# Moving snapshots and a copy ahead of the silus on ScalarE, squares of q and k into two homes, and two taps ahead of the joins

## The chip, the cores and the metric

The kernel runs on one core of one Trainium2 chip. The metric is the device time of one execution in microseconds (us); the number given for a version is the median of its runs. TensorE (PE) multiplies matrices into PSUM, VectorE (DVE), ScalarE (ACT) and GpSimd (POOL) work element by element, and SyncE (SP) issues most of the DMAs. All five run their own instruction streams in order and meet at semaphores.

## The reference, cut to what matters

Two transformer blocks follow each other on 512 latent tokens and 256 context tokens of width 1024, all in float32. The change touches the first layer of the first block alone, a gated delta rule in both directions (a "DeltaNet" mixer):

```
qkv = silu(centred_dwconv(p[..., :4096], conv_w))     # p = u @ w_in, five taps
z   = p[..., 4096:6144]
q, k = l2_norm(q), l2_norm(k)                         # 8 heads of 128, each used by two value heads
# chunks of 128 tokens here: invert (I + A), A strictly triangular; then scan over the chunks
o = rms_norm(o_forward + o_backward, o_norm_g)
y = (o * silu(z)) @ w_out
```

What follows it (attention, three kinds of attention in the second block, gates, a convolutional feed-forward part) is computed by code that the change leaves as it is.

## The kernel before, in words

**Layout.** Features lie on the 128 partitions and the 768 tokens along the row. The mixer is worked off in eight groups, j = 0 to 7; a group has one head of q, one of k and two of v, and two of z. A list of steps, written out by the generator `dn_order` (L259), is read by each engine's program, which picks from it the steps that it has a part in. The order of the list is therefore the order on every engine, and only semaphores move an engine against another. In the loop over j (L314) an iteration finishes group j and prepares group k = j + 1. It has three stretches.

**Stretch 1, products and solve (L322 to L361).** The projections are done by a fast scheme with seven products instead of eight, P1 to P7, for each pair of 128-row tiles (`pair_product`, L1329). Pair 0 of group k is q and k, pair 1 is its two v, pair 2 is the two z of group j. A product is eight matmuls of 385 columns. P1, P6, P7 and P4 add up in one PSUM bank: after each ScalarE copies the bank out (`pair_snap`, L2160), and the next of the four may not start before that copy is done. P2, P5, P7 and P3 also have an addition on VectorE (`pair_add`, L2759). In the same stretch ScalarE takes the square of the previous group's output (`osq`), the root of its mean (`sum_sq`, L2308), the silu of z (`zg`, L2212) and the silus of the two v tiles (`silu`, L2179); each of the two silu steps needs another table and loads back the one with Ln and Exp behind it. `gate_o` on VectorE scales the output by the root, and `finish` on TensorE transposes it (L1534). `blocks` (L2248) is a 96-row copy on ScalarE that waits for a DMA from DRAM (`blocks_in`, L1070), and VectorE's 15 steps `solve` (L2831) wait for it. `turn` transposes the two silued v tiles on TensorE, each followed by a copy on VectorE (L2797); the second transpose writes the same two banks and waits for the first copy.

**Stretch 2, joins (L399 to L403).** Nine rounds over six chunks: TensorE's small matmuls x, p and y for sizes 16, 32 and 64, each answered by copies or masks on ScalarE or VectorE. The list `behind` (L364) puts other work behind each round: the seven products of z, the 20 taps of the convolution of group k (`conv`, L2769, five for each of four tiles), the silu of q and k, and their norms. The norm of q (n = 0) and then of k (n = 1) is a square on VectorE (`norm_sq`, L2785), a sum over partitions on TensorE (`norm`, L1356), Ln and Exp on ScalarE (L2194) and a product on VectorE (`norm_x`, L2792). Both squares are written to the one buffer sqA, so k's square waits for q's sum.

**Stretch 3, scan (L419 to L448).** Six steps of a short chain between TensorE, VectorE and ScalarE, with the matrices of group k built beside it, and at its end P1 of the next group and the DMAs that bring group k's diagonal blocks to DRAM and back.

Of the kernel before, what the change touches and what calls it, by code (L numbers as in the profile page):

```python
# [16 lines left out]
LN_SET = "natural_log_exp_and_others"  # L17
# [241 lines left out]
def dn_order():  # L259
# [54 lines left out]
    for j in range(8):  # L314
# [5 lines left out]
            return [("pair_add", j, 2, name)]  # L320

        yield "clean", j  # L322
        if j:
            yield "zg", j - 1
        if j < 7:
            yield "silu", j, 2, 3
            yield from unit(k, 0, "P2") + unit(k, 0, "P6")
            if j:
                yield "sum_sq", j - 1
            yield "pair_add", k, 0, "P2"  # L330
            yield from unit(k, 0, "P5")
            yield "pair_add", k, 0, "P5"
            if j:
                yield "gate_o", j - 1
            yield from unit(k, 0, "P7")
            yield "pair_add", k, 0, "P7"
            yield "blocks", j
            yield from unit(k, 0, "P3")
            yield "solve", j, 1
            yield "pair_add", k, 0, "P3"  # L340
            yield from unit(k, 0, "P4")
            if j:
                yield "finish", j - 1
            for i in range(2, 9):
                yield "solve", j, i
            yield from unit(k, 1, "P1") + unit(k, 1, "P2") + unit(k, 1, "P6")
            for i in range(9, 16):
                yield "solve", j, i
            yield from unit(k, 1, "P5")
            yield "solved", j  # L350
            yield "pair_add", k, 1, "P2"
            if j:
                yield "fin_y", j - 1
            yield "turn", j, 0
            yield "turn", j, 1
            yield "pair_add", k, 1, "P5"
            yield from unit(k, 1, "P7")
            yield "pair_add", k, 1, "P7"
            yield from unit(k, 1, "P3")
            yield "pair_add", k, 1, "P3"  # L360
            yield from unit(k, 1, "P4")  # L361

            t = [x for n in range(4) for x in conv(k, n)]
            behind = [zh[:2] + t[:5], zh[2:4] + t[5:6], z_add("P2") + zh[4:7] + t[6:12],  # L364
                      [("silu", k, 0, 1)] + z_add("P5") + zh[7:10] + z_add("P7") + t[12:14], zh[10:12] + t[14:15],
                      z_add("P3") + zh[12:] + t[15:] + [("norm_sq", k, 0)],
                      [("norm", k, 0), ("norm_x", k, 0), ("norm_sq", k, 1)], [("norm", k, 1), ("norm_x", k, 1)], []]
            if k == 7:
                behind[8] = [("silu", 7, 2, 3), ("turn", 7, 0), ("turn", 7, 1)]
        else:  # L370


            p = [("mod_k", n, x) for n in (4, 5) for x in range(8)][1:] + zh
            out = [("out", 0, k, (0, 1)) for k in DN_OUT[:14]]
            behind = [p[27:], *(out[a:a + 2] for a in range(0, 14, 2)), []]
            behind[3] += [("zg", 7)]
            yield from p[:4]
            yield "sum_sq", 6
            yield "gate_o", 6
            yield "blocks", 7  # L380
            for i in range(1, 16):
                yield "solve", 7, i
                yield p[3 + i]
                if i == 2:
                    yield "finish", 6
                if i == 12:
                    yield "mod_turn", 4
                    yield "mod_turn", 5
                if i == 14:
                    yield "pair_add", 7, 2, "P2"  # L390
            yield "solved", 7
            yield "fin_y", 6
            yield from p[19:23]
            yield "pair_add", 7, 2, "P5"
            yield from p[23:25]
            yield "pair_add", 7, 2, "P7"
            yield from p[25:27]
            yield "pair_add", 7, 2, "P3"
# [127 lines left out]
def program(nc, D):  # L526

    ctx = ExitStack()
    with ctx:
# [83 lines left out]
        def raw_of(j, n):  # L613

            return conv_buf[(2 * (j % 3) + n) % 6]

        def conv_of(j, n):

# [558 lines left out]
        def tensor_program(e):  # L1177
# [176 lines left out]
                    leave_banks((f"pair_{event}", j, p), bank)  # L1354

            def norm(j, n):  # L1356
                e.wait_ge(*at("nrm_sq", j, n))
                take_banks(0, 1)
                e.matmul(ps[:, 0, :], ones, sqA[:, 0:512], start=True, stop=True)
                e.matmul(ps[:, 1, 0:256], ones, sqA[:, 512:768], start=True, stop=True).then_inc(*mark("nrm_pe", j, n))  # L1360
                leave_banks(("nrm_ln", j, n), 0, 1)

            def turn(j, h):
# [701 lines left out]
        def scalar_program(e):  # L2065
# [146 lines left out]
            def zg(j):  # L2212
                for event in ("c11", "c12", "c21", "c22"):
                    e.wait_ge(*at(f"pair_{event}", j, 2))
                e.activation(zg_of(j), zg_of(j), ACT.Silu).then_inc(*mark("z_silu", j))
                e.preload_act_table_set(LN_SET)

            def spread(j, c):

# [449 lines left out]
        def vector_program(e):  # L2669
# [115 lines left out]
            def norm_sq(j, n):  # L2785
                x = (qT, kT)[n][j % 2]
                e.wait_ge(*at("silu", j, n))
                if n:
                    e.wait_ge(*at("nrm_pe", j, 0))
                e.tensor_tensor(sqA, x, x, MUL).then_inc(*mark("nrm_sq", j, n))  # L2790

            def norm_x(j, n):  # L2792
                x = (qT, kT)[n][j % 2]
# [883 lines left out]
```

## Time and profile before

| | |
|---|---|
| median of 3 runs | 2994.41 us (2991.03 to 2996.15) |
| the profiled execution's own time | 2989.97 us |
| span of the profiled execution | 2988.2 us |
| mean granted TensorE clock | 0.973 of full speed |
| one iteration of the loop over j | 136.9 us (566.56 to 703.46, start of the same matmul group) |

Line numbers such as L1350 are lines of the kernel before. L2069 is the helper through which ScalarE copies, so snapshots, join copies and `blocks` all carry it; the shapes tell them apart (128x385 is a snapshot, 96x256 is `blocks` or `solved`). In a timeline a row is a group of equal instructions: its start, how long it lasted, and in brackets how long the engine had been idle before it and what it waited for. The "granted clock" of a stretch is 1.00 at 2.4 GHz and 0.50 at 1.2 GHz.

### The profile page before, as it was taken

How to read it: one execution, taken by the hardware profiler on the slowest of the kernel's cores; microseconds unless marked ns; L12 is line 12 of the kernel's file. 1: busy time of each engine (PE TensorE's matmuls, PEld its weight loads, DVE VectorE, ACT ScalarE, POOL GpSimd, SP SyncE). 2: the span in 40 equal slices, each digit the busy share in tenths (PEclk: the TensorE clock that was granted, in tenths of full speed). 3: DMA queues.
4: the chain of work that ended last, by engine and by line, in shares of the span. 5: the costliest groups of instructions: out<-in, count | busy, mean ns of one | idle time of the engine just before them, and what ended most of it. 6: DMA issues, size and time to landing. Idle time of an engine off the chain costs nothing.

```text
span 2988.2 us, 39117 instructions
## 1 busy us (share of the span) xinstructions
PE 2771.6 (93%) x15874; PEld 1910.7 (64%) x15874; DVE 1507.0 (50%) x3076; ACT 991.9 (33%) x2545; POOL 351.6 (12%) x268
## 2 busy tenths in 40 slices
PE   8798989898989979999999988999999999999998
PEld 3566666675757656764554434668776765588886
DVE  3565666666666653752333233543348421677733
ACT  1436364454636362202233222322224321211200
POOL 0220111101111110000000012123203220000031
PEclk9899999999999989999999999999999999999999
DMA  5110101111010114421100111111231211221220
GB/s 219 46 38 20 60 6 60 22 44 50 17 49 21 45 59 158 169 85 63 57 29 29 35 38 71 57 57 57 86 126 43 85 71 57 85 85 57 98 113 30
DMA packets 78132, 193.65 MB, mean 65 GB/s; under 512 B 56096, under 2 KB 61856, under 8 KB 66432
## 3 DMA queue, kind: packets, MB, share of 16 engines
q1 hardware_dynamic: 55520, 186.65, 17.3%
q10 hardware_dynamic: 22432, 4.49, 0.8%
q8 instruction: 126, 2.06, 0.3%
q14 instruction: 54, 0.44, 0.0%
HBM read 181.16 MB, written 9.96 MB: 64 GB/s over the span
## 4 chain that ended last, share of the span: by engine, by line
PE 81%; DVE 8%; ACT 8%; issue 1%; DMA 1%; ACTq 0%; SPq 0%; DVEq 0%
PE ps L1812 9%; PE ps L1350 9%; PE ps L2012 9%; PE ps L1264 7%; PE ps L1559 6%; PE ps L2040 4%; PE ps L1829 3%; PE ps L1952 3%; PE ps L1690 2%; DVE arena L2840 2%; ACT arena L2070 2%; PE ps L1418 2%; PE ps L1428 2%; PE ps L1440 2%; PE ps L1389 1%; PE ps L1702 1%
## 5 line engine op out<-in xcount | busy, mean ns | idle before, releaser
L2069 ACT ACTIVATE arena<-ps 64x64 f32<-64x64 f32 (+8 forms) x1011 | 320.3, 342 | 859.2 <-PE ps L1350 264.2
L1350 PE MATMUL ps<-arena 128*128 128x385 f32 x1232 | 431.4, 504 | 51.1 <-ACT arena L2069 51.1
L1350 PEld LDWEIGHTS ps<-arena 128*128 128x128 f32 x1232 | 234.4, 196 | 210.2 <-issue 69.6
L1812 PE MATMUL ps<-arena 128*128 128x256 f32 x1456 | 328.7, 380 | 2.0 <-ACT arena L2069 2.0
L1812 PEld LDWEIGHTS ps<-arena 128*128 128x128 f32 x1456 | 271.7, 191 | 40.2 <-issue 5.7
L2012 PE MATMUL ps<-arena 128*128 128x256 f32 x1176 | 254.7, 378 | 0.0
L2012 PEld LDWEIGHTS ps<-arena 128*128 128x128 f32 x1176 | 222.4, 189 | 32.5 <-issue 0.5
L1264 PE MATMUL ps<-arena 128*128 128x512 f32 x496 | 222.3, 607 | 14.7 <-DVE arena L3102 5.1
L1264 PEld LDWEIGHTS ps<-arena 128*128 128x128 f32 x496 | 96.0, 195 | 139.4 <-issue 130.2
L2070 ACT ACTIVATE arena<-ps,arena 128x128 f32<-128x128 f32 x544 | 157.1, 379 | 77.2 <-PE ps L1493 47.3
L1559 PE MATMUL ps<-arena 128*128 128x512 f32 (+1 forms) x512 | 170.3, 488 | 0.3 <-DVE arena L2931 0.3
L1559 PEld LDWEIGHTS ps<-arena 128*128 128x128 f32 x512 | 95.0, 189 | 64.9 <-issue 57.7
L2040 PE MATMUL ps<-arena 128*128 128x256 f32 x616 | 133.7, 379 | 1.2 <-DVE arena L3362 1.2
L2782 DVE SCALAR_TENSOR_TENSOR arena<-arena 128x770 f32<-128x770 f32 x128 | 131.2, 1025 | 3.8
L2040 PEld LDWEIGHTS ps<-arena 128*128 128x128 f32 x616 | 116.5, 189 | 18.2 <-DVE arena L3362 1.6
L2767 DVE TENSOR_TENSOR arena<-arena,ps 128x385 f32<-128x385 f32 x88 | 48.7, 553 | 147.4 <-ACT arena L2069 99.7
L2091 ACT ACTIVATE arena<-arena 128x768 f32<-128x768 f32 (+1 forms) x16 | 11.8, 737 | 259.0 <-DVE arena L3000 141.7
L2640 ACT ACTIVATE arena<-arena 128x512 f32<-128x512 f32 x44 | 33.4, 806 | 187.2 <-DVE arena L3346 187.2
L3506 POOL TENSOR_TENSOR arena<-arena 128x512 f32<-128x512 f32 x26 | 34.9, 1343 | 508.9 <-PE ps L1812 281.5
L2428 ACT ACTIVATE arena<-arena 128x128 f32<-128x128 f32 (+2 forms) x80 | 38.5, 482 | 162.4 <-DVE arena L3043 162.4
L1829 PE MATMUL ps<-arena 128*128 128x512 f32 x192 | 87.4, 597 | 0.0
L1952 PE MATMUL ps<-arena 128*128 128x512 f32 x192 | 85.7, 599 | 0.0
(360 smaller groups left out, 4322.5 us busy)
## 6 DMA issues: line engine op xcount, KB each, us to landing
arena<-in_ada_w SPq DMA_DIRECT2D x12, 2048.0 KB, 9.0
arena<-in_w_up SPq DMA_DIRECT2D x11, 2048.0 KB, 8.0
arena<-in_w_dil SPq DMA_DIRECT2D x9, 2048.0 KB, 7.8
arena<-in_w_dn SPq DMA_DIRECT2D x8, 2048.0 KB, 8.5
arena<-in_w_gate SPq DMA_DIRECT2D x6, 2048.0 KB, 8.1
arena<-in_w_down SPq DMA_DIRECT2D x4, 2816.0 KB, 9.5
arena<-in_att_in SPq DMA_DIRECT2D x5, 2048.0 KB, 8.0
arena<-in_w_z SPq DMA_DIRECT2D x8, 1024.0 KB, 4.9
```

What stands on the lines that cost most here:

```text
L1264: m = e.matmul(out, w[:, (k * m_tiles + x) * 128:(k * m_tiles + x) * 128 + 128], src(k), start=k == 0, stop=k == nk - 1)
L1350: m = e.matmul(ps[:, bank, 0:HALF_PAD], left[:, k], right[:, k], start=first and k == 0, stop=k == 3, skip_group_check=not first)
L1418: m = e.matmul(un64(ps[U, b, 0:256], u), quadrant(Yf, c, u, U, U), turner(U), start=True, stop=True)
L1559: m = e.matmul(o, lhsT, x, start=k == 0, stop=k == 15)
L1812: m = e.matmul(ps[:, bank, 0:256], left[:, k], right[:, k], start=first and k == 0, stop=k == 3, skip_group_check=not first)
L1829: m = e.matmul(ps[:, b, :], hv, w[:, k * 512:(k + 1) * 512], start=k == 0, stop=k == 7)
L1952: m = e.matmul(ps[:, b, :], w[:, a + k * 512:a + k * 512 + 128], y[:, k * 512:(k + 1) * 512], start=k == 0, stop=k == 3)
L2012: m = e.matmul(ps[:, b, 0:256], left[:, k], right[:, k], start=k == 0, stop=k == 3)
L2040: m = e.matmul(ps[:, b, 0:256], left[:, k], right[:, k], start=k == 0, stop=k == 10)
L2069: return e.activation(out, x, ACT.Copy)
L2070: return e.activation(out, x, ACT.Copy, scale=scale)
L2782: e.scalar_tensor_tensor(o, r[:, q:q + 770], cw[:, q:q + 1], o, MUL, ADD).then_inc(*(mark("tap", j, n, q) if q < 4 else mark("conv", j, n)))
```

## The change

The list of steps is reordered, one buffer gets a second home, and table loads go. TensorE's, SyncE's and GpSimd's instructions keep their order; only their waits can move.

1. `zg` of group j - 1 and the silus of group j's v tiles move from the start of stretch 1 to behind `blocks` (for j = 7 `zg` of group 6 too). The snapshots of P6 and P7, `sum_sq` and `blocks` thereby stand ahead of them on ScalarE.
2. `zg` no longer loads the Ln and Exp table back where a silu step follows it (j below 6), and that step then needs no load ahead of it: two table loads less in each of six iterations.
3. The square of k goes to oF (free between the store of an older output and the scan) instead of sqA, and no longer waits for q's sum, but for the DMA that stored the output of group j - 2. Both squares move ahead in the list, to behind the round x of size 32; the silu of q and k stands ahead of z's P6.
4. The addition of P5 (pair 1) moves ahead of the two `turn` steps, and the first two taps of group k's q to right behind them. The taps of q and k that follow move up in the list as well (k's first tap to behind the first round of joins); those of the two v tiles stay where they were.

```
         yield "clean", j
-        if j:
-            yield "zg", j - 1
         if j < 7:
-            yield "silu", j, 2, 3
...
             yield "blocks", j
+            if j:
+                yield "zg", j - 1
+            yield "silu", j, 2, 3
...
+            yield "pair_add", k, 1, "P5"
             yield "turn", j, 0
             yield "turn", j, 1
-            yield "pair_add", k, 1, "P5"
+            t = [x for n in range(4) for x in conv(k, n)]
+            yield from t[:2]
...
-            t = [x for n in range(4) for x in conv(k, n)]
-            behind = [zh[:2] + t[:5], zh[2:4] + t[5:6], z_add("P2") + zh[4:7] + t[6:12],
-                      [("silu", k, 0, 1)] + z_add("P5") + zh[7:10] + z_add("P7") + t[12:14], zh[10:12] + t[14:15],
-                      z_add("P3") + zh[12:] + t[15:] + [("norm_sq", k, 0)],
-                      [("norm", k, 0), ("norm_x", k, 0), ("norm_sq", k, 1)], [("norm", k, 1), ("norm_x", k, 1)], []]
+            behind = [zh[:2] + t[2:6], zh[2:4] + t[6:7], z_add("P2") + t[7:10] + [("silu", k, 0, 1)] + zh[4:7] + t[10:12],
+                      z_add("P5") + zh[7:10] + z_add("P7") + [("norm_sq", k, 0), ("norm_sq", k, 1)] + t[12:14],
+                      zh[10:12] + t[14:15], z_add("P3") + zh[12:] + t[15:],
+                      [("norm", k, 0), ("norm_x", k, 0)], [("norm", k, 1), ("norm_x", k, 1)], []]
...
             yield "blocks", 7
+            yield "zg", 6
...
+        def square_of(j, n):
+
+            return oF[:, 0:T_ALL] if j and n else sqA
...
             def norm(j, n):
+                s = square_of(j, n)
                 e.wait_ge(*at("nrm_sq", j, n))
                 take_banks(0, 1)
-                e.matmul(ps[:, 0, :], ones, sqA[:, 0:512], start=True, stop=True)
-                e.matmul(ps[:, 1, 0:256], ones, sqA[:, 512:768], start=True, stop=True).then_inc(*mark("nrm_pe", j, n))
+                e.matmul(ps[:, 0, :], ones, s[:, 0:512], start=True, stop=True)
+                e.matmul(ps[:, 1, 0:256], ones, s[:, 512:768], start=True, stop=True).then_inc(*mark("nrm_pe", j, n))
...
                 e.activation(zg_of(j), zg_of(j), ACT.Silu).then_inc(*mark("z_silu", j))
-                e.preload_act_table_set(LN_SET)
+                if j >= 6:
+                    e.preload_act_table_set(LN_SET)
...
             def norm_sq(j, n):
                 x = (qT, kT)[n][j % 2]
                 e.wait_ge(*at("silu", j, n))
-                if n:
-                    e.wait_ge(*at("nrm_pe", j, 0))
-                e.tensor_tensor(sqA, x, x, MUL).then_inc(*mark("nrm_sq", j, n))
+                if n and j >= 2:
+                    e.wait_ge(*at("y_out", j - 2))
+                elif n and not j:
+                    e.wait_ge(*at("nrm_pe", 0, 0))
+                e.tensor_tensor(square_of(j, n), x, x, MUL).then_inc(*mark("nrm_sq", j, n))
```

How the order moves is shown at three places. The first is ScalarE at the start of an iteration (j = 1), from the square of the output (128x1536) on. 128x385 is a snapshot (P6, then P7, then others), 128x12 is `sum_sq`, 96x256 is `blocks`, 128x1540 is `zg`, and 128x256 with 128x512 are the silus. Before:

```order
L2306 ACTIVATE arena<-arena 128x1536
L2215 ACT_TABLE_LOAD
L2215 ACTIVATE arena<-arena 128x1540
L2216 ACT_TABLE_LOAD
L2190 ACT_TABLE_LOAD
...
L2192 ACT_TABLE_LOAD
L2069 ACTIVATE arena<-ps 128x385
L2310 ACTIVATE arena<-arena 128x12
L2312 ACTIVATE arena<-arena 128x12
L2069 ACTIVATE arena<-ps 128x385
L2069 ACTIVATE arena<-arena 96x256
```

And in the changed kernel, whose lines stand a little lower:

```order
L2314 ACTIVATE arena<-arena 128x1536
L2076 ACTIVATE arena<-ps 128x385
L2318 ACTIVATE arena<-arena 128x12
L2320 ACTIVATE arena<-arena 128x12
L2076 ACTIVATE arena<-ps 128x385
L2076 ACTIVATE arena<-arena 96x256
L2222 ACT_TABLE_LOAD
L2222 ACTIVATE arena<-arena 128x1540
L2197 ACTIVATE arena<-arena 128x256
...
L2199 ACT_TABLE_LOAD
L2076 ACTIVATE arena<-ps 128x385 x3
```

Two snapshots, `sum_sq` and `blocks` passed the two silu steps, two of the four table loads are gone, and the snapshot of P4 (the first of the x3) stays behind them.

The second place is VectorE around the two copies of the transposed v (128x6x128), where 128x385 is a `pair_add` and 128x770 a tap. Before:

```order
L2931 SCALAR_TENSOR_TENSOR arena<-ps,arena 128x2x256
L2801 COPY arena<-ps 128x6x128 x2
L2767 TENSOR_TENSOR arena<-arena,ps 128x385 x3
L2779 TENSOR_SCALAR arena<-arena 128x770
L2782 SCALAR_TENSOR_TENSOR arena<-arena 128x770 x4
```

And in the changed kernel:

```order
L2941 SCALAR_TENSOR_TENSOR arena<-ps,arena 128x2x256
L2775 TENSOR_TENSOR arena<-arena,ps 128x385
L2811 COPY arena<-ps 128x6x128 x2
L2787 TENSOR_SCALAR arena<-arena 128x770
L2790 SCALAR_TENSOR_TENSOR arena<-arena 128x770
L2775 TENSOR_TENSOR arena<-arena,ps 128x385 x2
L2790 SCALAR_TENSOR_TENSOR arena<-arena 128x770 x3
```

One addition now stands ahead of the two copies, and two taps ahead of the other two additions.

The third place is VectorE late in the joins, where 128x256 x6 is the round x of size 32, 128x2x32 x12 the masks of size 32, 128x128 x6 the round x of size 64, and 128x768 a square or a `norm_x`. Before:

```order
L2848 COPY arena<-ps 128x256 x6
L2767 TENSOR_TENSOR arena<-arena,ps 128x385 x2
L2782 SCALAR_TENSOR_TENSOR arena<-arena 128x770 x2
L2854 TENSOR_TENSOR arena<-ps,arena 128x2x32 x12
...
L2790 TENSOR_TENSOR arena<-arena 128x768
L2859 COPY arena<-ps 128x128 x6
L2795 TENSOR_TENSOR arena<-arena 128x768
L2790 TENSOR_TENSOR arena<-arena 128x768
L2795 TENSOR_TENSOR arena<-arena 128x768
```

And in the changed kernel:

```order
L2858 COPY arena<-ps 128x256 x6
L2775 TENSOR_TENSOR arena<-arena,ps 128x385 x2
L2800 TENSOR_TENSOR arena<-arena 128x768 x2
L2790 SCALAR_TENSOR_TENSOR arena<-arena 128x770 x2
L2864 TENSOR_TENSOR arena<-ps,arena 128x2x32 x12
...
L2869 COPY arena<-ps 128x128 x6
L2805 TENSOR_TENSOR arena<-arena 128x768 x2
```

Both squares stand ahead of the masks of size 32, and none is left between the two `norm_x`.

## Rows read from the trace of the kernel before

**Rows 1.** The page's first part: busy time, share of the span and instructions of each engine

```profile
PE 2771.6 (93%) x15874; PEld 1910.7 (64%) x15874; DVE 1507.0 (50%) x3076; ACT 991.9 (33%) x2545; POOL 351.6 (12%) x268
```

**Rows 2.** Waits of PE, 200 to 1200 us: us in total, times, longest

```profile
PE ps L1350 <- ACT arena L2069: 47.8, 7, 7.6
PE ps L1359 <- DVE arena L2790: 17.0, 7, 3.4
...
PE ps L1369 <- DVE arena L2801: 11.1, 7, 1.7
PE ps L1540 <- DVE arena L2918: 7.6, 1, 7.6
```

**Rows 3.** Timeline of PE, stretch 1: start, us, engine, line, work, idle before

```profile
687.88 7.93 PE L1350 MATMUL ps<-arena 128*128 128x385 f32 x24
703.46 9.50 PE L1350 MATMUL ps<-arena 128*128 128x385 f32 x24 [7.64 <-ACT arena L2069]
...
726.93 0.87 PE L1369 MATMUL ps<-arena 128*128 128x128 f32 x6 [1.66 <-DVE arena L2801]
```

**Rows 4.** Timeline of ACT, start of stretch 1

```profile
695.66 1.49 ACT L2215 ACTIVATE arena<-arena 128x1540 f32<-128x1540 f32 x1
...
698.45 1.28 ACT L2190 ACT_TABLE_LOAD   x1
...
702.82 0.49 ACT L2069 ACTIVATE arena<-ps 128x385 f32<-128x385 f32 x1
...
708.20 0.63 ACT L2069 ACTIVATE arena<-arena 96x256 f32<-96x256 f32 x1
```

**Rows 5.** Timeline of DVE, stretch 1

```profile
694.38 1.75 DVE L2913 TENSOR_REDUCE arena<-arena 128x12 f32<-128x1536 f32 x1 [1.71 <-ACT arena L2306]
...
731.03 0.56 DVE L2767 TENSOR_TENSOR arena<-arena,ps 128x385 f32<-128x385 f32 x1 [1.77 <-ACT arena L2069]
```

**Rows 6.** SP's timeline, blocks_in; then line L1075, time from issue to landing

```profile
694.35 0.79 SPq L1075 DMA_DIRECT2D arena<-blocks  x2
...
DMA to landing us min/median/max: 1.9/2.0/2.2
```

**Rows 7.** Timeline of PE, joins

```profile
756.89 4.16 PE L1350 MATMUL ps<-arena 128*128 128x385 f32 x12
...
766.68 2.99 PE L1440 MATMUL ps<-arena 64*64 64x32 f32 x96
...
775.42 1.61 PE L1465 MATMUL ps<-arena 64*64 64x64 f32 x48
779.31 1.13 PE L1359 MATMUL ps<-arena 128*128 128x512 f32 x2 [2.28 <-DVE arena L2790]
...
784.44 1.70 PE L1508 MATMUL ps<-arena 128*128 128x128 f32 x8 [2.02 <-ACT arena L2069]
```

**Rows 8.** Timeline of DVE, joins

```profile
761.67 0.56 DVE L2767 TENSOR_TENSOR arena<-arena,ps 128x385 f32<-128x385 f32 x1 [2.63 <-ACT arena L2069]
...
764.25 1.66 DVE L2854 TENSOR_TENSOR arena<-ps,arena 128x64 f32<-128x64 f32 x12
...
772.74 0.95 DVE L2790 TENSOR_TENSOR arena<-arena 128x768 f32<-128x768 f32 x1
773.61 1.27 DVE L2859 COPY arena<-ps 128x128 f32<-128x128 f32 x6
777.43 0.96 DVE L2795 TENSOR_TENSOR arena<-arena 128x768 f32<-128x768 f32 x1 [2.55 <-ACT arena L2203]
```

**Rows 9.** Timeline of ACT, joins

```profile
747.65 4.17 ACT L2069 ACTIVATE arena<-ps 64x64 f32<-64x64 f32 x24 [5.81 <-PE ps L1440]
```

**Rows 10.** Busy time by stretch: us, PE, PEld, DVE, ACT, POOL busy, granted clock, DMA

```profile
648.50:651.90 3.40, 3.40 (x14) 2.86 (x14) 1.66 (x4) 3.34 (x13) 0.00 (x0) 0.51 0.00 0
...
725.00:729.00 4.00, 2.34 (x14) 1.57 (x13) 3.03 (x5) 0.00 (x0) 2.31 (x2) 1.00 0.51 67
...
703.40:706.50 3.10, 3.04 (x5) 1.84 (x6) 2.22 (x2) 0.32 (x2) 0.00 (x0) 0.50 0.00 0
```

## The prediction

> **What bounds the kernel now.** The page's first part gives TensorE 93% of the span, the next engine 50% [rows 1]; a modelled busy time says only that TensorE is the engine to watch. So the second view is its waits over the stretch in which the eight groups are worked off [rows 2]: each line names what TensorE waited for, the sum, how often and the longest. One line stands out, 47.8 us for snapshots on ScalarE, seven waits with 7.6 us as the longest. Next come 17.0 us for squares on VectorE (seven waits), 11.1 us for the copy of the transposed v (seven), and one wait of 7.6 us for `gate_o` in the last group. The third view is the timeline, for what stands in the queue of the engine that is waited for. In the iteration shown, TensorE ends P5 at 695.81 and stands still until 703.46 [rows 3]: P7 may not start before P6's snapshot, which ScalarE takes at 702.82, behind `zg` (695.66) and the v silus with their loads (from 698.45) [rows 4]. P6 itself was finished after two thirds of that group of 24, at about 693.2. The last view is the granted clock by stretch [rows 10].
>
> **Moving the snapshots, `sum_sq` and `blocks` up (the main term).** The square of the output ends at about 694.4, when VectorE's reduction starts [rows 5]. P6's snapshot then runs from there to 694.9, 0.49 us by its row [rows 4]. TensorE wants it at 695.8, so it no longer waits; 0.9 us is the slack. The two small `sum_sq` steps wait for the reduction, which ends at 696.1, and are over by 697. P7 ends a third of 7.93 us after 695.81, at 698.5; its snapshot is done at 699.1, P3 hides it (P4 starts at 701.1). So 7.64 us go in each of six iterations (j = 1 to 6; group 0 lies before this stretch and has no `zg`): **45.8 us**. The other 2.0 us of the 47.8 belong to a wait in the last group, and stay.
>
> **The clock behind that gap.** The 24 matmuls after the wait took 9.50 us, the 24 before it 7.93 [rows 3], and the granted clock in their first 3.1 us was 0.50, the 1.2 GHz level [rows 10]. TensorE had stood still for 7.64 us before. With the gap gone I give back 9.50 - 7.93 = 1.57 us six times, **9.4 us**.
>
> **What now stands behind `blocks`.** `blocks` waits for a DMA that is issued at 694.35 and landed after 2.0 us (2.2 at most) [rows 6], so at 696.6; it is not late for its new place at 699.1, and its 0.63 us end at 699.7. `zg` with its load takes 2.8 us (695.66 less the load's 1.28, to 1.49 behind it), the silus took 4.37 us with two loads (698.45 to 702.82) and take 3.09 with one [rows 4]. P4's snapshot therefore comes at 705.6 and is done at 706.1. P4 itself is done at 695.8 + 7.9 = 703.7; the next user of its bank is P2 of pair 1, behind the transposes of `finish` and behind P1 (2.65 us), so not before 706.4. Slack 0.3 us plus the transposes: cost nothing; if that cover goes, each microsecond costs six. `fin_y` needs `zg` only behind the 15 solves. The solves begin with `blocks` and are paced by P3's addition, both earlier by as much as TensorE is. The 12 table loads that go (two in six iterations, 1.28 us each) lie on ScalarE beside all this and are counted in these sums, not added. The Trainium skill prices a switch higher ("ScalarE: Activation LUTs", What ACT_TABLE_LOAD costs): about 1.28 us for the load and 1.38 us more for a drain. By it the two loads left in this chain would make P4's snapshot 2.8 us later and the sum some 7 to 15 us smaller. The rows speak against it: two loads and four activations of the silus fit into 4.37 us [rows 4].
>
> **The two squares.** k's square was released by q's sum, and TensorE stood 2.28 us before k's sum [rows 7]. Now both squares are ready long before. k's Ln on ScalarE then waits for q's `norm_x`, which ends at 778.4 [rows 8], and for k's sum, which can follow the round w (775.42 + 1.61 = 777.0) at 778.6 instead of 779.31 + 1.6 = 780.9. ScalarE's copies of the last round, for which the scan waits 2.02 us [rows 7], move by the same 2.3 us, so that wait stays as it is and the gap is a gain: all **17.0 us** of rows 2. The new wait for the store of an output of two groups before costs nothing: that store is issued in stretch 1, and the square comes late in stretch 2.
>
> What the early squares push: they stand on VectorE behind P7's addition, at 762.2, and take 2 x 0.88 us; two taps and the masks of size 32 follow, so the masks start at 766.0 instead of 764.25 [rows 8]. TensorE wants the first mask, 0.3 us later, at 766.68 [rows 7]: slack 0.35 us, the tightest place of the change, I cost it at nothing. The copies of size 64 start 0.9 us later (one square less ahead of them in exchange), at 774.5, the first is there at 774.8, and TensorE wants it at 775.42. The silu of q and k now runs ahead of z's P6 snapshot: ScalarE's round y ends at 751.8 [rows 9], plus 4.37 and 0.49 gives 756.7; z's P7 starts four matmuls into the group at 756.89, at 758.3 [rows 7]. Slack 1.6 us, nothing.
>
> **P5's addition ahead of the turns.** It pushes the copy that TensorE waits for by 0.48 us (0.56 by its row, less the overlap) in seven iterations: **3.4 us lost**, the wait growing from 1.66 to 2.14 us. The two taps behind it fill time in which VectorE waited 1.77 us for the next addition [rows 5]; that addition comes at most 0.6 us later and only z's products use its bank: nothing.
>
> **Last group.** `gate_o` waited behind `zg` and two loads, 4.1 us; now only behind the reduction, 1.8 us. Of its 7.6 us wait 2.3 go, part of it at low clock: **2.0 us**.
>
> **The clock elsewhere**, the least known term. In each of the seven scans one stretch of 3.4 us ran at 0.51 [rows 10], a loss of half, 1.7 us, 11.9 in all. Ahead of it TensorE had stood 2.28 and then 2.02 us with 3 us of work between; the wait of 1.66 us at the turns left it at 1.00 [rows 10]. After the change 2.02 remains, alone, and the other becomes 2.14. Bounds: all 11.9 come back; or they stay and seven more such losses come at the turns, -11.9. I take **3 us** back, nearer the middle, since both remaining waits lie between a row that kept the clock and one that lost it.
>
> **Sum.** 45.8 + 9.4 + 17.0 + 2.0 + 3 - 3.4 = 73.8 us. Against the profiled execution's own 2989.97 us (span 2988.2) that is 2916; the median of the three runs is 4.4 us higher, so I predict **2920.6 us**. A measurement of this kernel tells 0.2% (6 us) from no change.
>
> **Rivals.**
> - *The clock stays full.* Both waits of about 2.1 us turn out too short to bring it down: 8.9 us more come back, 2911.7 us. For it: 1.66 us did nothing. Against it: the drop followed a wait of 2.02 us. The Trainium skill would have it so ("TensorE: Matmul & The Clock Gate", Why this matters for your kernels: it warns of idle gaps longer than both of these). The trace agrees at 1.66 us; at 2.02 us it is open, since 2.28 stood close ahead. Chance 0.2.
> - *k's norm gains nothing.* ScalarE's chain of Ln, Exp and copies sets the scan's start and q's part alone is as late as before; the wait moves from the sum to the scan. 17.0 us less: 2937.6. Against it: the end of q's `norm_x` at 778.4. Or, near it in time, P4's snapshot or the masks of size 32 are late by 1 to 2 us each iteration: 7 to 15 us less, 2928 to 2936. Chance 0.14 together.
> - *The new queue behind `blocks` makes it slower.* ScalarE is in order, and the silus, P4's snapshot and through it P2 now wait for a DMA round trip that they did not wait for before. From a landing about 3 us after 696.6 on, each microsecond costs one per iteration; to lose all 73.8 us over six iterations takes 12.3 us more, a landing 17 us after the issue, and at 20 us the time would be 3012. No landing of the sixteen took over 2.2 us, and the blocks' DMAs keep their order. Chance 0.02.
> - *The change doesn't do what it says:* P6's snapshot is held by another of its waits (the taps of the v tiles of the group before), so only the squares and the last group gain: 2980. Those taps end a whole scan earlier; chance 0.02.
>
> **Numbers.** My forecast has 0.62. Its own range is 2909 (clock back, turns unchanged) to 2934 (clock term at its worst). Taking in the first two rivals the range is 2906 to 2938. Faster 0.97, within 0.2% 0.01, slower 0.02.
>
> **What would show it.** Right: no wait of 7.6 us before L1350's successor (of the 47.8 us some 2 are left), none for squares, turns at 2.1 us, 12 fewer table loads, an iteration of 124 to 126 us instead of 136.9. Wrong: a wait at P2 of pair 1 for ScalarE (P4's snapshot), at the round y of size 32 for VectorE (masks), a wait over 3 us at the scan's start, or ScalarE idle ahead of the 96x256 copy for a DMA.

## The result and the profile after

The changed kernel takes 2918.34 us (median of 4 runs, 2914.14 to 2919.43) against 2992.84 us before (median of 4); the ratio is 0.9747, with a 95% interval of 0.9730 to 0.9764. It is **faster by 74.5 us**; 2920.6 was forecast. In the profiled execution the span fell from 2988.2 to 2912.3 us, by 75.9.

The page's first part for the changed kernel (busy time, share of the span, instructions):

```profile
PE 2754.4 (95%) x15874; PEld 1901.5 (65%) x15874; DVE 1499.1 (51%) x3076; ACT 975.2 (33%) x2533; POOL 360.0 (12%) x268
```

Beside [rows 1] two numbers speak. ScalarE has twelve instructions fewer, the table loads. TensorE has the same number of instructions and 17.2 us less busy time: the same matmuls ran at a higher clock (mean granted clock 0.983 against 0.973).

TensorE's waits over the eight groups, 200 to 1150 us, all that are over 1 us (total, times, longest):

```profile
PE ps L1376 <- DVE arena L2811: 13.9, 7, 2.1
PE ps L1515 <- ACT arena L2076: 12.8, 7, 2.0
PE ps L1376 <- ACT arena L2198: 5.9, 1, 5.9
PE ps L1547 <- DVE arena L2928: 5.3, 1, 5.3
PE ps L1406 <- ACT arena L2243: 5.0, 7, 0.7
PE ps L1356 <- ACT arena L2076: 2.5, 1, 2.5
```

Read against [rows 2]: the snapshots' line (L1350, now L1356) fell from 47.8 to 2.5 us and its seven waits to one; the squares' line (17.0 us) is gone; the turns (L1369, now L1376) rose from 11.1 to 13.9, the last group's `gate_o` (L1540, now L1547) fell from 7.6 to 5.3. The wait at the start of the scan (L1515) is still 2.0 us in six of its seven times. These four lines come to 83.5 us before and 21.7 now, 61.8 less. Two others rose, the wait at the scan by 0.6 us and, in the last group, the turns' wait for the silu of v (the third line above) from 4.8 to 5.9; with them 60.1 us of waiting went. The lower busy time is 17.2, together 77.3, near the 75.9 of the span.

The timeline of TensorE at the start of an iteration, the answer to [rows 3]:

```profile
523.56 15.71 PE L1356 MATMUL ps<-arena 128*128 128x385 f32 x48
539.10 1.47 PE L1547 MATMUL ps<-arena 128*128 128x128 f32 x12
540.41 10.52 PE L1356 MATMUL ps<-arena 128*128 128x385 f32 x32
550.77 0.82 PE L1376 MATMUL ps<-arena 128*128 128x128 f32 x6
553.72 0.88 PE L1376 MATMUL ps<-arena 128*128 128x128 f32 x6 [2.13 <-DVE arena L2811]
```

P2 to P4 are one row of 48 matmuls without a gap, at full clock (twice 7.9 us). From the second turn here to the next one, at 678.07, an iteration takes 124.4 us (125.8 the one before), as forecast, instead of 136.9. The only idle time left in these rows is 2.13 us at the second turn. ScalarE in the same stretch, the answer to [rows 4]:

```profile
528.54 1.48 ACT L2314 ACTIVATE arena<-arena 128x1536 f32<-128x1536 f32 x1 [3.06 <-DVE arena L2835]
529.93 0.47 ACT L2076 ACTIVATE arena<-ps 128x385 f32<-128x385 f32 x1
...
534.12 0.49 ACT L2076 ACTIVATE arena<-ps 128x385 f32<-128x385 f32 x1 [1.72 <-PE ps L1356]
534.51 0.64 ACT L2076 ACTIVATE arena<-arena 96x256 f32<-96x256 f32 x1
535.17 1.28 ACT L2222 ACT_TABLE_LOAD   x1
536.46 1.49 ACT L2222 ACTIVATE arena<-arena 128x1540 f32<-128x1540 f32 x1
...
540.92 0.49 ACT L2076 ACTIVATE arena<-ps 128x385 f32<-128x385 f32 x1
```

P6's snapshot follows the square at once and is done at 530.4, 1.0 us before P5 ends. `blocks` runs right behind P7's snapshot and waits for no DMA. P4's snapshot ends at 541.4, and P2 of pair 1 wants the bank at 543.0. In the joins VectorE shows the tight place, the answer to [rows 8]:

```profile
588.93 1.99 DVE L2800 TENSOR_TENSOR arena<-arena 128x768 f32<-128x768 f32 x2
590.85 2.07 DVE L2790 SCALAR_TENSOR_TENSOR arena<-arena 128x770 f32<-128x770 f32 x2
592.83 1.66 DVE L2864 TENSOR_TENSOR arena<-ps,arena 128x64 f32<-128x64 f32 x12
```

and TensorE's round y of size 32 begins at 593.46 in its own timeline, without a wait:

```profile
593.46 2.99 PE L1447 MATMUL ps<-arena 64*64 64x32 f32 x96
```

### The profile page after: what moved, and what is told of

Same layout as the page of the kernel before. It is cut to its first block, busy times and chain, and to the rows that moved or that the text cites. A ratio compares the mean times of both kernels' runs of the same rounds, so it can differ in the third digit from the quotient of the medians.

```text
span 2912.3 us, 39099 instructions
## 1 busy us (share of the span) xinstructions
PE 2754.4 (95%) x15874; PEld 1901.5 (65%) x15874; DVE 1499.1 (51%) x3076; ACT 975.2 (33%) x2533; POOL 360.0 (12%) x268
## 4 chain that ended last, share of the span: by engine, by line
PE 84%; DVE 8%; ACT 5%; issue 1%; DMA 1%; ACTq 0%; SPq 0%; DVEq 0%
PE ps L1356 11%; PE ps L1819 10%; PE ps L2019 9%; PE ps L1270 7%; PE ps L1566 6%; PE ps L2047 4%; PE ps L1836 3%; PE ps L1959 3%; PE ps L1697 2%; DVE arena L2850 2%; PE ps L1425 2%; PE ps L1447 2%; PE ps L1435 2%; PE ps L1396 2%; PE ps L1709 2%; PE ps L1536 1%
## 5 line engine op out<-in xcount | busy, mean ns | idle before, releaser
L1356 PE MATMUL ps<-arena 128*128 128x385 f32 x1232 | 421.8, 496 | 5.9 <-ACT arena L2076 5.9
L1356 PEld LDWEIGHTS ps<-arena 128*128 128x128 f32 x1232 | 230.7, 192 | 159.1 <-issue 13.6
L2790 DVE SCALAR_TENSOR_TENSOR arena<-arena 128x770 f32<-128x770 f32 x128 | 137.6, 1075 | 3.3
```

The lines of the kernel that those rows point to most:

```text
L1356: m = e.matmul(ps[:, bank, 0:HALF_PAD], left[:, k], right[:, k], start=first and k == 0, stop=k == 3, skip_group_check=not first)
L2790: e.scalar_tensor_tensor(o, r[:, q:q + 770], cw[:, q:q + 1], o, MUL, ADD).then_inc(*(mark("tap", j, n, q) if q < 4 else mark("conv", j, n)))
```

## The experiments

All medians stand beside runs of the kernel before on the same chip. `+` and `-` are against the kernel named.

| version | median, us | ratio to before, 95% interval |
|---|---|---|
| changed kernel | 2918.3 | 0.9747 (0.9730 to 0.9764) |
| snap_only | 2928.4 | 0.9780 (0.9762 to 0.9798) |
| squares_only | 2966.2 | 0.9910 (0.9895 to 0.9925) |
| loads_only | 2978.4 | 0.9957 (0.9943 to 0.9970) |
| one_home | 2938.2 | 0.9824 (0.9810 to 0.9839) |
| blocks_last | 2947.6 | 0.9849 (0.9829 to 0.9869) |
| four_loads | 2921.1 | 0.9756 (0.9731 to 0.9782) |
| third_square | 2922.3 | 0.9762 (0.9742 to 0.9783) |
| p5_back | 2913.4 | 0.9731 (0.9712 to 0.9749) |
| turn_between | 2897.9 | 0.9679 (0.9665 to 0.9694) |
| norm_last | 2917.9 | 0.9749 (0.9730 to 0.9769) |
| norm_filled | 2904.3 | 0.9712 (0.9698 to 0.9725) |
| changed kernel again (one execution) | 2916.7 | |

### The snapshots and blocks alone

```
# against the kernel before
         yield "clean", j
-        if j:
-            yield "zg", j - 1
         if j < 7:
-            yield "silu", j, 2, 3
...
             yield "blocks", j
+            if j:
+                yield "zg", j - 1
+            yield "silu", j, 2, 3
...
             yield "blocks", 7
+            yield "zg", 6
...
-                e.preload_act_table_set(LN_SET)
+                if j >= 6:
+                    e.preload_act_table_set(LN_SET)
```

> The kernel before with the first two parts alone: zg and the v silus behind blocks, two table loads fewer in six iterations; squares, taps and P5's addition as before. My theory: the six waits of 7.64 us for P6's snapshot go (45.8 us), the matmuls behind them run at full clock (9.4 us), gate_o in the last group comes 2 us earlier: 57 us less than before, about 2936. The waits for the squares (17.0 us) and for the turned v (11.1 us, 1.66 each) stay. Rival, k's norm gave most: less than 45 us come off and new waits stand where the 7.64 us were. Rival, the silus merely move the wait: P4's snapshot is late and P2 of pair 1 waits for ScalarE.

It took 2928.4 us, 65.5 less than before instead of 57. Its waits, 200 to 1150 us:

```profile
PE ps L1360 <- DVE arena L2792: 17.0, 7, 3.4
PE ps L1370 <- DVE arena L2803: 11.1, 7, 1.7
PE ps L1509 <- ACT arena L2070: 11.1, 7, 2.0
PE ps L1541 <- DVE arena L2920: 5.3, 1, 5.3
...
PE ps L1351 <- ACT arena L2070: 2.0, 1, 2.0
```

The snapshots' waits are gone and the other two lines are to the tenth those of before, so this part is worth what the theory says, and neither rival holds. The 8 us on top are only in part explained. Of the pairs of waits of 2.28 and 2.02 us ahead of a scan one of six no longer lost the clock (1.00 at 491 us), which is worth 1.7 us; the others still did, as at 364 us:

```profile
364.30:367.70 3.40, 3.40 (x12) 2.97 (x12) 1.29 (x4) 3.36 (x13) 0.00 (x0) 0.50 0.02 5
491.00:494.40 3.40, 3.40 (x23) 2.71 (x22) 1.80 (x5) 3.30 (x13) 0.00 (x0) 1.00 0.02 5
```

(The columns are explained in the next section.) TensorE's busy time fell by 19.1 us in all, part of it outside the mixer, in code that no version touches.

### The squares alone

```
# against the kernel before: the third part of the change (second home, both squares early,
# silu of q and k early), with all five of q's taps behind the first round
-            behind = [zh[:2] + t[:5], zh[2:4] + t[5:6], z_add("P2") + zh[4:7] + t[6:12],
...
+            behind = [zh[:2] + t[:6], zh[2:4] + t[6:7], z_add("P2") + t[7:10] + [("silu", k, 0, 1)] + zh[4:7] + t[10:12],
+                      z_add("P5") + zh[7:10] + z_add("P7") + [("norm_sq", k, 0), ("norm_sq", k, 1)] + t[12:14],
...
```

> The kernel before with the third part alone: k's square in its second home and both squares ahead of the masks of size 32, silu of q and k ahead of z's P6, no taps ahead of the joins. My theory: the seven waits for the square go, 17.0 us, the waits of 2.02 us at the scan stay, and 0 to 12 us of clock come back: 2964 to 2976. Rival, k's norm gains nothing because ScalarE's chain sets the scan's start: the wait before the scan grows from 2.02 to 4.3 us and the time is that of before, 2993.

It took 2966.2 us, 27.7 less than before: the whole wait and 10.7 us of clock. Two stretches of it, one behind the wait ahead of the scan and one around the wait for the snapshot (us from and to, length, busy times of PE, PEld, DVE, ACT, POOL, granted clock, DMA share and GB/s):

```profile
498.70:502.10 3.40, 3.39 (x21) 2.71 (x22) 1.70 (x4) 3.29 (x13) 0.00 (x0) 1.00 0.02 5
...
549.40:556.20 6.80, 2.88 (x5) 1.69 (x6) 2.22 (x2) 4.13 (x9) 0.00 (x0) 0.51 0.00 0
```

Behind the 2.02 us alone the clock is 1.00, where before it was 0.51 [rows 10], and so it is in all six iterations that have this wait; behind the 7.64 us it still falls. The wait at the scan's start did not grow (12.1 us in six), so the rival falls. The two parts alone give 65.5 + 27.7 = 93 us, 19 more than the whole change. The traces explain some 11 us of the difference. The stretches at low clock of 1.7 us loss each, ahead of the scans, are seven before, six in `snap_only` and none in `squares_only`; the changed kernel has three, and one at a turn. So the parts alone get eight back and the whole change only four, less one that is new at the turn: 8.5 us. P5's addition, which neither part has, costs 2.8 us. Why `squares_only` keeps the clock in every iteration and the changed kernel doesn't is open.

### One home again

```
# against the changed kernel
-            return oF[:, 0:T_ALL] if j and n else sqA
+            return sqA
...
-                if n and j >= 2:
-                    e.wait_ge(*at("y_out", j - 2))
-                elif n and not j:
-                    e.wait_ge(*at("nrm_pe", 0, 0))
+                if n:
+                    e.wait_ge(*at("nrm_pe", j, 0))
...
-        ... z_add("P7") + [("norm_sq", k, 0), ("norm_sq", k, 1)] + t[12:14],
+        ... z_add("P7") + [("norm_sq", k, 0)] + t[12:14],
-        [("norm", k, 0), ("norm_x", k, 0)], ...
+        [("norm", k, 0), ("norm_x", k, 0), ("norm_sq", k, 1)], ...
```

> The changed kernel with sqA as the one home of both squares again: q's square stays early, k's waits for q's sum and stands behind q's norm_x as before the change. My theory: the wait of 2.28 us before k's sum is back in seven iterations, 17 us and up to 10 us of clock: 2934 to 2945. Rival, the early place does it and not the second home: within 3 us of the changed kernel.

2938.2 us, inside what was expected, and the line of before is back as it was:

```profile
PE ps L1366 <- DVE arena L2798: 17.0, 7, 3.4
```

k's square can't be early without a second home, and with q's alone early the wait is what it was.

### The table loads alone, and all four of them in the new place

```
# loads_only, against the kernel before: in zg
-                e.preload_act_table_set(LN_SET)
+                if j >= 6:
+                    e.preload_act_table_set(LN_SET)

# four_loads, against the changed kernel: the reverse
```

> The kernel before with nothing but the two table loads gone in six iterations (zg and the v silus stay at the start). My theory: P6's snapshot stands right behind them, so the wait of 7.64 us falls by two loads of 1.28 us to 5.1 us: 15.4 us less than before, 2978, the clock behind it still falls. Rival, a switch costs twice a load: 5.3 us less each, 32 us, 2961. Rival, the loads lie beside other work: 2993.

> The changed kernel with zg's reload of the Ln and Exp table back, so that the v silus need their own load again: four table loads in the chain behind blocks instead of two. My theory, from the rows of the changed kernel: two loads of 1.28 us make P4's snapshot end at 544.0 instead of 541.4 in the iteration at 524 us, and TensorE wants its bank for P2 of pair 1 at 543.0: a new wait of 1.0 us in six iterations, 6 us, about 2924. Rival, a switch of tables costs twice a load (a drain of 1.4 us behind each): the snapshot ends 2.8 us later still, the wait is 3.8 us, 23 us, 2941. Rival, the removed loads lie wholly beside other work: 2918, no new wait.

`loads_only` took 2978.4 us, 13.2 less than before, and the snapshots' line reads

```profile
PE ps L1350 <- ACT arena L2069: 32.2, 7, 4.9
```

that is 15.6 us less wait, six times two loads of 1.28 and a little more. `four_loads` took 2921.1 us, 2.8 above the changed kernel (too little to tell apart by the times), but its timeline shows the expected wait of 1.0 us, at P2 of pair 1:

```profile
545.18 2.75 PE L1356 MATMUL ps<-arena 128*128 128x385 f32 x8
548.93 8.03 PE L1356 MATMUL ps<-arena 128*128 128x385 f32 x24 [1.00 <-ACT arena L2076]
```

It costs less than six microseconds because the later P2 takes some of the turns' waits away (9.0 us in eight instead of 15.5). A switch costs one load here. By the dearer price of the Trainium skill ("ScalarE: Activation LUTs", What ACT_TABLE_LOAD costs: about 2.66 us) the two would have made this wait 1.00 + 2 x 1.38 = 3.8 us, an estimate from that page's figure. The slack of P4's snapshot is 1.6 us, and two loads fill it.

### blocks behind the silus

```
# against the changed kernel
-            yield "blocks", j
             if j:
                 yield "zg", j - 1
             yield "silu", j, 2, 3
+            yield "blocks", j
```

> The changed kernel with blocks put behind zg and the v silus on every engine (P7's snapshot stays ahead of them). My theory: the 96-row copy comes 5.8 us later, the first solve and with it P3's addition wait for it; TensorE first waits some 3 us for the bank of P3 before the transposes of finish, then longer at the turns, 4.5 to 5 us in all per iteration, some 30 us, and 0 to 10 us of clock on top: 2948 to 2958. Rival, only the snapshots mattered: within 5 us of the changed kernel.

2947.6 us, 29 above the changed kernel. The waits, 170 to 1150 us:

```profile
PE ps L1547 <- DVE arena L2775: 16.9, 6, 2.8
PE ps L1376 <- DVE arena L2811: 15.1, 8, 4.5
```

`finish` waits 2.8 us for the bank of P3's addition in six iterations, as expected. The turns were expected to wait longer, and did so in two iterations (4.47 and 3.00 us), not in all. The rest of the loss is clock: TensorE's busy time is 2768.2 us against 2754.4, 13.8 more, where 0 to 10 had been expected. So the copy `blocks` must go ahead together with the snapshots; snapshots alone would have given up two fifths of the gain.

### A third square

```
# against the changed kernel
+                if n:
+                    e.tensor_tensor(oF[:, T_ALL:2 * T_ALL], x, x, MUL)
                 e.tensor_tensor(square_of(j, n), x, x, MUL).then_inc(*mark("nrm_sq", j, n))
```

> The changed kernel with one more square of k on VectorE, next to the two, written to a part of oF that nobody reads: a doubled suspected cost. My theory: the masks of size 32 start 0.87 us later, the slack is 0.35 us, so TensorE waits about 0.5 us for VectorE before the round y of size 32 in seven iterations, 3.6 us, about 2922. Rival, the slack is really larger (TensorE's work between hides it): no wait for VectorE at that round and no change. Rival, VectorE is the bound of the joins already: the full 0.87 us each, 6 us, and a wait at the round w of size 64 too.

2922.3 us, 4 above the changed kernel, and one new line among the waits:

```profile
PE ps L1447 <- DVE arena L2866: 3.8, 7, 0.6
```

Seven waits of 0.55 us for 0.87 us more work: the slack is the 0.3 us that the timelines show. There is none at the round w. The change has left 0.3 us of the joins' slack on VectorE.

### P5's addition back, and a product between the turns

```
# p5_back, against the changed kernel
-            yield "pair_add", k, 1, "P5"
             yield "turn", j, 0
             yield "turn", j, 1
+            yield "pair_add", k, 1, "P5"

# turn_between, against the changed kernel
             yield "turn", j, 0
+            yield from unit(k, 1, "P7")
             yield "turn", j, 1
             t = [x for n in range(4) for x in conv(k, n)]
             yield from t[:2]
-            yield from unit(k, 1, "P7")
```

> The changed kernel with P5's addition put back behind the two turns; the two taps stay ahead of the other additions. My theory: the wait for the first copy of v falls from 2.13 to 1.66 us, 0.48 us in seven iterations: 3 us less than the changed kernel, about 2915. If waits of about 2.1 us are what lets the clock fall, there are also fewer stretches at 0.50 in the mixer, each worth 1.7 us. Rival: the addition was moved up because something waits for it, then a wait for VectorE appears at z's products or the joins and the time rises.

> The changed kernel with P7 of pair 1 between the two turns, so that TensorE multiplies while VectorE copies the first v. My theory: the waits for the copy (13.9 us, seven) go, since eight matmuls take 2.65 us and the wait is 2.13: about 14 us less than the changed kernel, 2904; with fewer low-clock stretches in the mixer up to 5 us more. Rival, the solves bound the iteration: the joins then wait for the DMA that brings the inverses back, and nothing or little is gained.

`p5_back` took 2913.4 us, 4.9 less than the changed kernel, with 12.3 us in eight waits at the turns (170 to 1150 us) instead of 15.5. That part of the change is a loss of 3 us and of one low stretch at a turn (at 679 us in the changed kernel, none in `p5_back`), and nothing waited for the addition; the medians alone, whose ranges overlap (2908 to 2916 and 2914 to 2919), would hardly tell it. The waits at the turns in the changed kernel and in `p5_back`:

```profile
PE ps L1376 <- DVE arena L2811: 15.5, 8, 2.1
```

```profile
PE ps L1376 <- DVE arena L2811: 12.3, 8, 1.7
```

`turn_between` took 2897.9 us, 20 less than the changed kernel and **the fastest version of the study**. One wait of 1.1 us for VectorE is left at the turns, and in the iteration shown there is none:

```profile
545.59 2.76 PE L1356 MATMUL ps<-arena 128*128 128x385 f32 x8
548.18 0.82 PE L1376 MATMUL ps<-arena 128*128 128x128 f32 x6
548.84 5.35 PE L1356 MATMUL ps<-arena 128*128 128x385 f32 x16
554.11 3.02 PE L1425 MATMUL ps<-arena 64*64 64x64 f32 x96
```

The joins follow without a gap, so the way of the inverses through DRAM still has slack; the rival falls. The 6 us more than forecast are not the fewer low stretches that had been hoped for. None is left at a turn, but five of the six waits ahead of a scan now lose the clock, against three in the changed kernel. Two equal waits, with the clock behind each:

```profile
600.70 1.92 PE L1515 MATMUL ps<-arena 128*128 128x128 f32 x8 [2.02 <-ACT arena L2076]
846.80 1.20 PE L1515 MATMUL ps<-arena 128*128 128x128 f32 x8 [2.02 <-ACT arena L2076]
```

```profile
601.20:604.60 3.40, 3.40 (x15) 2.87 (x15) 1.48 (x4) 3.17 (x12) 0.00 (x0) 0.55 0.00 0
847.00:850.40 3.40, 3.40 (x23) 2.70 (x23) 1.73 (x5) 3.30 (x13) 0.00 (x0) 1.00 0.00 0
```

### k's norm later, two tries

```
# norm_last, against turn_between
-        [("norm", k, 0), ("norm_x", k, 0)], [("norm", k, 1), ("norm_x", k, 1)], []]
+        [("norm", k, 0), ("norm_x", k, 0)], [], [("norm", k, 1), ("norm_x", k, 1)]]

# norm_filled, against turn_between: TensorE's sum there, the rest behind the scan's first step
+        [("norm", k, 0), ("norm_x", k, 0)], [], [("norm", k, 1)]]
...
-            after = [[("spread", k, 1), ("kn", k)], [("decay", k, 0), ("decay", k, 1)],
+            after = [[("norm_root", k, 1), ("spread", k, 1), ("norm_x", k, 1)],
+                     [("kn", k), ("decay", k, 0), ("decay", k, 1)],
```

> The version with P7 between the turns, and k's norm put behind the round y of size 64 instead of before it, so that its sum on TensorE fills the wait of 2.02 us ahead of the scan. My theory: the wait at the scan's start goes (12.9 us in seven), but ScalarE's Ln and Exp of k then stand ahead of the first copies of the scan, which come 1 to 1.5 us late, so a new wait of about 1 us appears at the scan's first outputs or at the transposes of k: 4 to 10 us less than 2897.9, about 2891; if the wait of 2.02 us is what lets the clock fall in five iterations, no stretch at 0.50 is left ahead of a scan, part of that sum. Rival: k's norm is on the critical chain, and everything gained comes back as a wait for q and k: 2898 or more.

> The version with P7 between the turns, k's sum behind the round y of size 64 on TensorE, and k's Ln, Exp and norm_x only behind the first copies and additions of the scan (ScalarE and VectorE no longer stand in the scan's way as in norm_last). My theory: norm_last failed because VectorE's norm_x, which waits for ScalarE's Exp, stands ahead of the scan's first products; with it behind them the wait of 2.02 us at the scan's start is filled, 0.6 us stay at the round y: 1.4 us in seven iterations, 10 us less than 2897.9, and up to 8 us more if the five low-clock stretches at the scans go too: 2880 to 2890. Rival, ScalarE is full in the first scan steps (the spreads), and k's Ln and Exp push them: waits for ScalarE or VectorE of 1 to 3 us inside the scan, 2895 or more.

Both missed. `norm_last` took 2917.9 us, 20 more than `turn_between`: the wait moved behind the first products of the scan and grew, because VectorE's `norm_x` stood in the queue ahead of the scan's product and waited for Exp.

```profile
606.76 1.05 PE L1515 MATMUL ps<-arena 128*128 128x128 f32 x8
611.08 2.08 PE L1524 MATMUL ps<-arena 128*128 128x256 f32 x4 [3.27 <-DVE arena L2884]
```

`norm_filled` took 2904.3 us, 6 more than `turn_between`. The wait at the scan's start is gone, and three smaller ones (170 to 1150 us) took its place:

```profile
PE ps L1515 <- DVE arena L2877: 12.5, 7, 1.8
PE ps L1396 <- ACT arena L2076: 6.9, 7, 1.0
...
PE ps L1484 <- ACT arena L2076: 4.0, 7, 0.6
```

The second step of the scan waits for VectorE, the decays for the copy of k's transposes, and the round y for ScalarE: 23 us in place of 12.9. That is the rival, with VectorE beside ScalarE. No order was found in which this chain costs less than the 2.02 us ahead of the scan.

### The changed kernel once more

> The changed kernel itself, one more execution with a profile. My theory: all waits of TensorE in the mixer are the same to 0.1 us, but the stretches at 0.50 behind the wait of 2.02 us fall in other iterations or in another number, since the same wait lost the clock at 483 us and kept it at 609 us. Rival: the stretches fall in the same iterations, so the program alone sets them.

The waits in the groups are the same to 0.1 us. But so are the places where the clock falls: the stretch behind the scan's start at 483 us ran at 0.53 in the first profile and at 0.51 in the second, and the three others (at 358, 679 and 860 us) are in both too.

```profile
484.60:488.00 3.40, 3.40 (x15) 3.00 (x15) 1.23 (x4) 3.37 (x13) 0.00 (x0) 0.53 0.00 0
```

```profile
484.60:488.00 3.40, 3.40 (x15) 3.22 (x15) 1.35 (x4) 3.30 (x12) 0.00 (x0) 0.51 0.02 5
```

My expectation was wrong and the rival right for the mixer, as far as two executions tell. For the whole program it isn't: at 2334 us, in the code that the change leaves, the clock was 1.00 in the first profile and 0.58 in the second.

## Why the prediction was right

- **Snapshots moved up, 45.8 us.** Measured 45.3 on that line, and 45.8 in `snap_only`. The place in the queue, the slack of 0.9 us (1.0 measured) and the silent part of `blocks` (no wait for its DMA) came out as worked.
- **The clock behind that gap, 9.4 us.** TensorE's busy time on the line of the products fell on the two pages from 431.4 to 421.8 us, 9.6, net of the one new low stretch at a turn.
- **Behind blocks, nothing.** P4's snapshot had 1.6 us of slack where at least 0.3 was claimed; `four_loads` shows where it ends. The Trainium skill's dearer price of a table switch ("ScalarE: Activation LUTs", What ACT_TABLE_LOAD costs) is not what these runs show: 1.28 us each in the changed timeline, and 15.6 us for twelve loads in `loads_only`.
- **Two squares, 17.0 us.** All of it on their own line, the wait at the scan's start unchanged at 2.02. But in the last group TensorE's next wait, for the silu of v, is 5.9 us instead of 4.8 (6.8 in `squares_only`): 1.1 us are given back, for which the sum has no term. The masks' slack was given as 0.35 us and is 0.3 (`third_square`).
- **P5's addition, 3.4 us lost.** 2.8 measured, the wait at 2.13 against 2.14 forecast.
- **Last group, 2.0 us.** 2.3 measured as a wait, but the low-clock stretches of this group cost 7.7 us (3.5, 2.6 and 1.6) against 5.5 before (3.8 and 1.7). The loss of a stretch is its busy time times what its granted clock lacks of 1.00.
- **The clock elsewhere, 3 us.** This is the term that was mis-sized, and its reason did not hold. Ahead of the scans seven stretches had lost 1.7 us each; three are left, and one is new at a turn, so 5.1 us came back. The step that failed is that the loss was divided by the length of the wait: 2.28, 2.02 and 2.14 us were taken to lie between a wait that keeps the clock and one that loses it. The same 2.02 us kept it in six of six iterations of `squares_only` and lost it in five of six of `turn_between`. Within the changed kernel it lost it at 483 us (0.53) and not at 609:

```profile
608.90:612.30 3.40, 3.40 (x21) 2.71 (x22) 1.70 (x4) 3.29 (x13) 0.00 (x0) 1.00 0.00 0
...
679.10:682.50 3.40, 3.40 (x7) 1.87 (x6) 2.48 (x3) 0.00 (x0) 0.00 (x0) 0.54 0.99 253
```

The second row is a turn of the changed kernel, behind a wait of about 2.1 us. Counted over the six iterations that have these waits:

| version | waits ahead of a scan, us | lost the clock there | wait at a turn, us | lost it there |
|---|---|---|---|---|
| before | 2.28 and 2.02 | 6 of 6 | 1.7 | none |
| snap_only | 2.28 and 2.02 | 5 of 6 | 1.7 | none |
| squares_only | 2.02 | none | 1.7 | none |
| changed kernel | 2.02 | 3 of 6 | 2.1 | one |
| p5_back | 2.02 | 3 of 6 | 1.7 | none |
| turn_between | 2.02 | 5 of 6 | none | none |
| third_square | 2.02 | 4 of 6 | 2.1 | two |
| one_home | 2.28 and 1.8 or less | 6 of 6 | 2.1 | four |

(The numbers of waits are the longest ones; where the clock falls behind the first of a pair, the second is shorter. The seventh stretch of before and a sixth of `snap_only` lie in the last group, behind a wait of 3.35 us.) So the first rival, that both waits are too short to lower the clock, does not hold, and the Trainium skill's advice ("TensorE: Matmul & The Clock Gate", Why this matters for your kernels), which warns only of longer gaps, doesn't cover these rows. What decides between a 2.02 us that costs the clock and one that doesn't was not settled.

That the total came within 2.3 us is in part luck. The low-clock stretches of the last group (2.2 us), its longer wait for the silu of v (1.1) and the clock elsewhere (2.1 above the forecast) largely cancel, and of the 17.2 us of busy time nearly 4 lie outside the mixer, in code that the change leaves and whose low stretches differ between two executions of the same kernel. Two figures of the prediction are slightly off by its own numbers: the clock term at its worst gives 2935.5 us, not 2934, and a landing 20 us after the issue 3009, not 3012.

The other rivals fell: k's norm did gain, and no wait for the DMA of `blocks` shows. What the two taps ahead of the joins are worth by themselves was not tried; they lie in VectorE's idle time, and in `squares_only`, which lacks them, no round of the joins waited for VectorE.

## What to carry to other kernels

When an engine waits for a copy that is short in itself, list what stands ahead of it in the copying engine's queue, and ask of each item who waits for it: here 8 us of silus that nobody needed for 20 us stood ahead of a half-microsecond snapshot. Move the short step, and with it every step of the same queue that starts a long chain (the 96-row copy ahead of the solves was worth 29 us). A wait for one buffer's copy between two equal steps can be filled with a product that is needed anyway: this one-line move gave 20 us more. Where a trace shows that equal waits cost the clock in some iterations only, put the clock into a forecast as a range, and don't add up what two edits gain alone.

## What had not been expected of the hardware

The length of a wait of TensorE did not tell whether the clock falls behind it: behind 2.02 us it fell in none, three, four or five of six iterations, depending on the version. The stretches at 1.2 GHz of the mixer lay at the same microseconds of the program in two executions, though the waits ahead of them don't differ from those of the other iterations. And gains of clock don't add: 65.5 and 27.7 us alone, 74.5 together.
